# Mixture-of-experts pass of a transformer kernel: three column tiles (32, 32, 64 wide) instead of four tiles of 32

## The reference

```python
D_MODEL, SEQ, MOE_EXPERTS, MOE_TOPK, MOE_D_FF = 1024, 256, 32, 2, 512

def expert_block(args):
    x_blk, e = args
    return (jax.nn.silu(x_blk @ w_gate[e]) * (x_blk @ w_up[e])) @ w_down[e]

yb = lax.map(expert_block, (xb, blk_e)).reshape(P, D)
y = jax.ops.segment_sum(yb.astype(f32) * slot_w[:, None], slot_tok, num_segments=T + 1)[:T]
```

## Time and profile before

| | |
|---|---|
| median of 3 runs | 1024.76 us (1020.86 to 1026.21) |
| the profiled execution's own time | 1021.17 us |
| its span in the trace | 1019.4 us |
| mean granted TensorE clock | 0.986 of full |
| PE matmul busy | 967.9 us, 95% of the span |
| PE weight loads busy | 537.6 us, 53% |
| VectorE busy | 417.3 us, 41% |
| ScalarE busy | 187.9 us, 18% |
| bytes moved | 302.49 MB, mean 297 GB/s |

### The profile page before, as it was taken

The page is one execution under the profiler, slowest core; times in us unless marked ns, Lnnn a source line. Parts: engine busy times, 40 slices in busy tenths (PEclk is TensorE's granted clock), DMA queues, the critical chain, the costliest instruction groups (busy, mean ns, idle before and its releaser), DMA issues.

```text
span 1019.4 us, 15507 instructions
## 1 busy us (share of the span) xinstructions
PE 967.9 (95%) x6429; PEld 537.6 (53%) x6429; DVE 417.3 (41%) x806; ACT 187.9 (18%) x424; POOL 30.1 (3%) x92
## 2 busy tenths in 40 slices
PE   8999999999999999999999899999889998898996
PEld 7788866576666665468764533333223232332332
DVE  4576556175555565402222754622223122222213
ACT  2425244110000001214342101111001101000111
POOL 8200000000000000000000000000000000000000
PEclk9999999999999999999999999999999999999999
DMA  9443022785666689543144899999999999999994
GB/s 354 179 152 104 3 83 83 283 335 211 284 281 281 283 347 395 240 172 104 62 166 165 311 422 427 427 425 429 427 425 427 428 428 426 427 428 427 416 413 190
DMA packets 30529, 302.49 MB, mean 297 GB/s; under 512 B 6016, under 2 KB 6144, under 8 KB 12032
## 3 DMA queue, kind: packets, MB, share of 16 engines
q1 hardware_dynamic: 30464, 301.53, 72.2%
HBM read 300.47 MB, written 1.05 MB: 296 GB/s over the span
## 4 chain that ended last, share of the span: by engine, by line
PE 71%; DMA 18%; SPq 6%; DVE 2%; ACT 1%; issue 1%; DVEq 0%
PE PS L1669 11%; PE PS L1270 10%; PE PS L1265 9%; PE PS L2015 8%; PE PS L1718 8%; DMA slot<-in_moe_w_up_dram 8%; SPq L680 6%; PE PS L2034 6%; DMA AR<-in_moe_w_up_dram 4%; DMA XH<-in_moe_w_up_dram 4%; PE PS L1991 3%; PE PS L1500 2%; PE PS L1616 2%; DMA slot<-in_moe_w_down_dram 2%; PE PS L1966 1%; PE PS L1712 1%
## 5 line engine op out<-in xcount | busy, mean ns | idle before, releaser
L1669 PE MATMUL PS<-XH,slot 128*128 128x256 f32 x512 | 113.3, 379 | 1.7 <-DVE XH L2554 0.9
L1669 PEld LDWEIGHTS PS<-XH,slot 128*128 128x128 f32 x512 | 97.1, 190 | 21.3 <-issue 8.9
L1265 PE MATMUL PS<-XH,slot 128*128 128x256 f32 x432 | 97.8, 383 | 1.6 <-DMA slot<-in_w_in_dram 1.6
L1265 PEld LDWEIGHTS PS<-XH,slot 128*128 128x128 f32 x432 | 80.7, 190 | 14.2 <-DMA slot<-in_w_in_dram 1.8
L2034 PE MATMUL PS<-slot,ATT 128*32 128x512 f32 x576 | 67.0, 619 | 9.6 <-DMA slot<-in_moe_w_up_dram 9.6
L2015 PE MATMUL PS<-slot,ATT 128*32 128x512 f32 x544 | 65.3, 606 | 7.2 <-issue 4.3
L1270 PE MATMUL PS<-slot,XH 128*128 128x256 f32 (+4 forms) x224 | 71.7, 476 | 0.0
L2015 PE MATMUL PS<-slot,MASKS 128*32 128x512 f32 x576 | 64.3, 594 | 1.8 <-DMA slot<-in_moe_w_down_dram 1.4
L2603 DVE SCALAR_TENSOR_TENSOR AR<-AR 128x384 f32<-128x384 f32 (+1 forms) x112 | 59.9, 613 | 0.0
L1991 PE MATMUL PS<-AR,DIAG 128*128 128x512 f32 x120 | 57.6, 605 | 0.0
L1270 PEld LDWEIGHTS PS<-slot,XH 128*128 128x128 f32 x224 | 42.0, 190 | 26.1 <-issue 14.8
(11 more groups left out here) (477 smaller groups left out, 1172.4 us busy)
## 6 DMA issues: line engine op xcount, KB each, us to landing
slot<-in_moe_w_up_dram SPq DMA_DIRECT2D x18, 2048.0 KB, 30.6
slot<-in_w_ffn_dram SPq DMA_DIRECT2D x16, 2048.0 KB, 8.4
slot<-in_moe_w_gate_dram SPq DMA_DIRECT2D x16, 2048.0 KB, 36.3
slot<-in_moe_w_down_dram SPq DMA_DIRECT2D x16, 2048.0 KB, 36.4
AR<-in_ada_w_dram SPq DMA_DIRECT2D x16, 1536.0 KB, 14.1
AR<-in_moe_w_gate_dram SPq DMA_DIRECT2D x9, 2048.0 KB, 34.0
AR<-in_moe_w_down_dram SPq DMA_DIRECT2D x8, 2048.0 KB, 35.9
AR<-in_moe_w_up_dram SPq DMA_DIRECT2D x8, 2048.0 KB, 34.3
```

The costliest lines, as they stand in the source:

```text
L1265: ins = pe.matmul(dst, w[:, c * width + col:c * width + col + n], HT[:, c, :], start=(c == 0), stop=(c == KC - 1))
L1669: ins = pe.matmul(PS[:, b, (f % 2) * T:(f % 2 + 1) * T], slots[s][:, c * 512 + f * P:c * 512 + (f + 1) * P], HT[:, c, :], start=(c == 0), ...
```

## The change

The last two entries of SKEWED, slots 64 to 95 and 96 to 127, both of the larger expert, become one entry, slots 64 to 127. The larger expert's 96 slots are then one tile of 32 (slots 32 to 63) and one of 64 (slots 64 to 127). QUARTERS, and with it pass 0, stays as it was. All users of SKEWED follow: `project`, `project_back`, `project_part`, `project_back_part` and `up_part`.

```diff
             QUARTERS = tuple((k * FEW, (k + 1) * FEW, k) for k in range(QUAD))
-            SKEWED = ((0, FEW, 0), (FEW, 2 * FEW, 1), (2 * FEW, 3 * FEW, 1), (3 * FEW, P, 1))
+            SKEWED = ((0, FEW, 0), (FEW, 2 * FEW, 1), (2 * FEW, P, 1))
```

## The result

The changed kernel takes 1356.04 us in the median of four runs (1354.52 to 1359.25), against 1023.51 us before in the same comparison. The ratio is 1.327 with a 95% interval of 1.324 to 1.329: a third slower. The profiled execution took 1354.52 us, its span is 1352.8 us.

What follows compares the result with a forecast made beforehand. It took PE and the weight transfers as candidate bounds before, PE alone after: 13 passes of 51.9 us from 614.66, then 56.0 for the last pass, 10.0 tail and 1.8 around the span give 1357 us, range 1265 to 1400.

Steps and rivals of the forecast that it cites:

- The exclusion: In mixed chunks, 32- and 64-column tiles can't stream together; 64-column records start about 0.5 us behind the 32-column ones.
- The chunk: Each mixed product chunk takes 1.98 us where 0.86 stood: two doubled streams plus two changes of width, +1.12 us.
- The change of width: Switching tile width between groups on PE costs 0.13 us, bounds 0.11 and 0.19.
- The sum: 24 chunks make a pair pass 51.9 us on PE; 13 passes, last pass and tail give a span of 1355.5 us.
- the weights' pace: Weight transfers set 29.1 us for each of ten passes before; run spread was put down to this and nothing added.
- The DMA share: Share of DMA use in the pair-pass stage after the change: near 0.56, from 29.1 / 51.9.
- Widths that don't exclude each other: Rival: the 64-column tile starts with the others, mixed groups stay at 0.43 us, time 1021 to 1026 us; chance 0.15.
- a tax without exclusion: Rival: streams overlap in mixed chunks but each change costs 0.13 us; pass 31.3 us, time 1069 us; chance 0.03.
- no overlap at all: Rival: mixed-group records run in program order, one more stream per chunk, 144 us more, 1501 us; chance 0.03.
- Fewer changes by PE's own choice: Rival: PE runs several chunks' 32-column work before one change; at the limit 89 us less, 1268 us; chance 0.07.
- some 4 us: PE slack in each of the ten passes that wait for weights; dearer PE work up to that costs nothing.
- the first rival: Rival that widths don't exclude each other; decided by a mixed group under about 0.52 us, hidden by slack; chance 0.15.

Runs made afterwards that it cites:

- the run sorted by width: Changed kernel with each accumulation running all chunks of the 32-column tiles first, then all of the 64-column tile: 1281.68 us, ratio 1.254.
- three mixed chunks: Kernel before with mixed widths in the first three chunks of each pair pass's gate projection, last pass included: 1032.38 us, ratio 1.009.
- up alone: Kernel before with mixed widths only in the up projection of passes 1 to 13: 1099.07 us, ratio 1.075.
- the run with idle columns: Kernel before with one 32-column and one 64-column tile, columns 32 to 63 idle, in all but each accumulation's first and last chunk: 1231.72 us, ratio 1.203.
- two mixed chunks: Kernel before with mixed widths in the first two chunks of the gate projection of passes 1 to 12: 1021.24 us, ratio 1.000.

## Why the prediction was right

**The exclusion.** Predicted: 64-column records about 0.5 us behind the 32-column ones, two groups for each one before. Measured: 0.53 us, and again for two tiles that share no column. By the Trainium skill, TensorEngine Tiling (Array Packing), section Tiling Modes, a change of mode drains the array. The runs agree: 0.86 us a chunk for equal widths, and turns of 1.95 to 1.98 us for mixed ones, with idle columns between them too.

**The chunk.** Predicted 1.98 us, measured 15.88 / 8 = 1.985. The change of width, taken as 0.13 from one row between bounds of 0.11 and 0.19, came out at 0.13. That it was so close is luck in part: the row of 128 to 32 columns was taken because it lay between the ends, and the middle of the bounds, 0.15, would have given 344 x 2 x 0.02 = 14 us more.

**The sum.** Pass: 51.9 predicted, 51.93 measured. From gate of pass 1 (628.48 - 15.88 = 612.6 in the chain) to gate of pass 14 (1287.59) it is 675.0, where 674.8 was predicted:

```profile
605.66 22.82 PE PS L2015 x112
628.48 15.88 PE PS L2034 x48
```

The start of the gate of pass 14 is in the timeline of PE:

```profile
1287.59 1.05 PE L2015 MATMUL PS<-AR,ATT 128*32 128x512 f32 x4
```

From there to the last scatter, 1342.8 - 1287.6 = 55.2 us against 56.0. Most of the 0.8 us lies in the down parts: by the timelines they took about 7.6 us before, not 8 x 0.86 = 6.9, as they already stood beside other widths, and 15.9 after, some 0.7 less growth than 8 x 1.12. The tail is 10.0 us as before. The span came out 2.7 us under the predicted 1355.5: 2.1 because gate of pass 1 began at 612.6 in place of 614.66, which the change does not touch, and 0.8 in the last pass, less 0.2 in the passes.

**What it left out or explained wrongly, and what luck did.** The prediction is for a profiled time of 1357 us; that execution took 1354.52, and the median of all four is 1356.04. It added nothing for the spread of the runs, which it put down to the weights' pace. That reason is wrong: the weights no longer set the pace, and the four runs still spread over 4.7 us, with the granted clock falling from 0.998 in the shortest span (1352.8 us) to 0.992 in the longest (1357.5 us). The traces before and after, which differ by 2 us at pass 1, already differ far ahead of the change: from 100 to 200 us the granted clock is 0.98 in the one and 1.00 in the other. The sum also has no term for the gap at the loop's way back, 4.28 us idle in the kernel before and some 6 us with its slow restart. It would have counted with PE as the bound. It is absent in the changed kernel, which nothing in the prediction foresaw.

**What else was to be seen.** The clock is 1.00 in the window, as said. No wait for a weight transfer is left. The DMA share is 0.61, not 0.56; the rate, 244 / 427 = 0.57, is what was worked out. Why the share stands above the rate stays open; it bears on nothing here.

**The rivals.** Widths that don't exclude each other, a tax without exclusion, and no overlap at all are excluded by the timeline. Fewer changes by PE's own choice does not happen: the run sorted by width shows what it would have been worth, 74 us (1356 to 1282, medians of two sets), where 89 were given as the limit.

**A step that was wrong, though outside the sum.** The prediction gave the weights' slack as "some 4 us" in each of ten passes, and the expectation for three mixed chunks rested on that. The slack is one sum over the passes 1 to 13: 366.35 us, less 13 x 25.03 for PE, less some 5.7 for the gap at the loop's way back with its restart, leaves 35.3 us. Work in the first three passes draws on it too. Three chunks in 13 passes are 43.7 us, 8.4 too many, and the last pass keeps 3.4 - 1.4 = 2: 10.4 against the measured 9.7 (1032.38 - 1022.73). Two chunks in 12 passes are 26.9 and cost nothing. The threshold for the first rival, 0.52 us per mixed group, was for the same reason too high: 35.3 / 13 = 2.7 us a pass gives 0.43 + 2.7 / 48 = 0.49. At the measured 0.99 us a group that decided nothing. The same gap explains the 4 us by which up alone missed: its chain has 5.3 us more in that one pass, less 1.7 for the shorter projection.

## What to carry to other kernels

Float32 column tiles of 32 and 64 columns ran side by side here only with tiles of their own width; a merge that saves a call but mixes widths turns one group into two, plus 0.13 us for every change. Other pairs of widths within a group were not run. If widths must be mixed, sort the calls by width over a whole accumulation; here that gave back 74 of 333 us. Count the slack beside a stream of transfers as one sum over all passes that the buffers connect, and look in it for gaps at loop ends that the transfers hide now and that come out when they no longer do. Whether such a gap is there can change with the number of instructions in the loop, so count them before and after a change.

## What the runs showed of the hardware that was not expected

Records are not started in strict program order across tiles of one width. The two records of a call stand behind one another in the program, as the turns of two and two in the run with idle columns bear out. Yet three other tiles' first records start within 0.01 us of the first tile's, whose second comes 0.43 us later. Across a change of width nothing is pulled ahead, even into idle columns. Dropping a quarter or half of a chunk's records at equal width left a projection at 6.87 us and moved the medians by 0.2%. And PE stood idle for 3.3 to 4.3 us once at the loop's way back in five of the eleven kernels. The products behind it took 1.7 to 3.1 us longer (8.77 against 7.07 with up alone, 12.19 against 9.12 with two mixed chunks), with a granted clock, over the gap and these products, of 0.86 with up alone and 0.79 with two mixed chunks. The gap was absent with slow work in front, and in all kernels whose second round loads no instructions.
